# A decoder block on one core: operand start addresses, one-product sums, the start, and two groups of TensorE work moved

## What is computed

```python
xn = rmsnorm(x, norm1_g)
h  = x + mix(sig(g_conv) * conv(xn) + sig(g_attn) * attention(xn))   # conv ends in a layernorm
hn = rmsnorm(h, norm2_g)
q  = hn @ w_q                       # queries: 8 heads, 2 halves of 128
s  = einsum(q, sub_keys); top 16 of each half -> 16 of 128 x 128 experts, gate = softmax
act = gelu(u_tab[e] . hn) * gate    # 16384 experts in u_tab and v_tab
y  = h + sum(act * v_tab[e])
```

## Time and profile before

| | |
|---|---|
| median of 3 runs | 995.61 us (995.38 to 995.79) |
| the profiled execution | 996.06 us, of which the span of the trace is 994.3 us |
| TensorE busy | 989.9 us (100% of the span), 7822 records |
| VectorE, ScalarE, GpSimd busy | 773.4, 507.4, 464.6 us |
| bytes moved | 181.95 MB, mean 183 GB/s |

### The profile page before, as it was taken

One profiled execution on the slowest core, in us unless ns is written; L12 is line 12 of the kernel. 1 busy time (PEld: TensorE's weight loads), 2 busy tenths in 40 slices (PEclk: granted clock), 3 DMA queues, 4 the chain that ended last, 5 costly groups with the idle time before them and its releaser, 6 DMA issues.

```text
span 994.3 us, 21854 instructions
## 1 busy us (share of the span) xinstructions
PE 989.9 (100%) x7822; PEld 917.3 (92%) x7822; DVE 773.4 (78%) x1304; ACT 507.4 (51%) x789; POOL 464.6 (47%) x198
## 2 busy tenths in 40 slices
PE   9999999999999999999999999999999999999998
PEld 9998999999999999999999999888888888888887
DVE  6899784868899995097777777988888877676764
ACT  6654877644554444644444444444444445544443
POOL 4554466656689999874444444000000004344442
PEclk9999999999999999999999999999999999999999
DMA  7684445554455455555555545545545545555552
GB/s 263 226 272 153 147 148 183 201 191 149 161 200 190 169 211 190 190 186 177 182 176 178 177 170 170 191 169 174 180 174 174 183 171 191 191 189 199 183 206 87
DMA packets 52619, 181.95 MB, mean 183 GB/s; under 512 B 5943, under 2 KB 9155, under 8 KB 52452
## 3 DMA queue, kind: packets, MB, share of 16 engines
q1 hardware_dynamic: 52292, 181.16, 53.0%
q10 hardware_dynamic: 288, 0.27, 0.1%
HBM read 180.33 MB, written 3.43 MB: 185 GB/s over the span
## 4 chain that ended last, share of the span: by engine, by line
PE 98%; ACT 1%; DVE 0%; issue 0%; POOL 0%; ACTq 0%; POOLq 0%
PE bank L1218 53%; PE bank L1528 35%; PE bank L1477 3%; PE bank L1320 2%; PE bank L1233 1%; PE bank L1452 1%; PE bank L1242 1%; PE bank L1554 1%; PE bank L1336 1%; PE bank L1359 0%; PE bank L1347 0%; ACT hi L335 0%; DVE lo L354 0%; PE bank L1249 0%; PE bank L1297 0%; PE bank L1287 0%
## 5 line engine op out<-in xcount | busy, mean ns | idle before, releaser
L354 POOL TENSOR_TENSOR lo<-raw,hi 128x1024 fp32r<-128x1024 f32 x184 | 461.7, 2523 | 515.6 <-ACT hi L335 515.0
L335 ACT CAST hi<-raw 128x1024 fp32r<-128x1024 f32 x332 | 348.2, 1050 | 214.4 <-PE bank L1528 186.2
L1218 PE MATMUL bank<-norm_space,hi 128*128 128x256 f32 x2624 | 452.3, 278 | 0.0
L1218 PEld LDWEIGHTS bank<-norm_space,hi 128*128 128x128 f32 x2624 | 395.6, 188 | 1.5 <-issue 0.8
L1218 PE MATMUL bank<-norm_space,lo 128*128 128x256 f32 x1312 | 362.8, 277 | 0.0
L1528 PE MATMUL bank<-hi,norm_space 128*128 128x512 f32 x1008 | 273.8, 391 | 0.0
L1218 PEld LDWEIGHTS bank<-norm_space,lo 128*128 128x128 f32 x1312 | 246.4, 188 | 0.0
L1528 PEld LDWEIGHTS bank<-hi,norm_space 128*128 128x128 f32 x1008 | 187.9, 188 | 38.6
L354 DVE TENSOR_TENSOR lo<-raw,hi 128x1024 fp32r<-128x1024 f32 x148 | 187.3, 1266 | 27.2 <-ACT hi L335 27.2
L1528 PE MATMUL bank<-lo,norm_space 128*128 128x512 f32 x504 | 155.5, 390 | 0.0
L1145 DVE TENSOR_TENSOR norm_space<-act,norm_space 128x256 fp32r<-128x256 f32 x128 | 111.6, 875 | 48.8 <-ACT norm_space L665 48.8
(11 more groups left out here) (183 smaller groups left out, 653.6 us busy)
## 6 DMA issues: line engine op xcount, KB each, us to landing
raw<-u_tiles SPq DMA_DIRECT2D x128, 512.0 KB, 3.3
raw<-v_tiles SPq DMA_DIRECT2D x128, 512.0 KB, 3.3
raw<-front SPq DMA_DIRECT2D x76, 512.0 KB, 3.8
toeplitz<-bias_row SPq DMA_DIRECT2D x6, 384.0 KB, 7.4
bias<-toeplitz SPq DMA_DIRECT2D x12, 128.0 KB, 3.7
resid<-x_t SPq DMA_DIRECT2D x2, 512.0 KB, 4.8
qk<-sub_keys SPq DMA_DIRECT2D x1, 1024.0 KB, 7.5
y<-act SPq DMA_DIRECT2D x3, 256.0 KB, 2.0
```

The lines of the kernel that those rows point to most:

```text
L335: act_e.copy(hi[:, s, :], raw[:, s, :]).then_inc(hi_ready, 1)
L354: eng.tensor_tensor(lo[:, s, :], raw[:, s, :], hi[:, s, :].bitcast(F32), ALU.subtract)\
L1218: ins = pe.matmul(dst, w_[:, s, u * P:(u + 1) * P], x_[:, k, :], start=first and i == 0 and p_ == 0, stop=last and i == n - 1 and p_ == 2)
```

## The change

- **Starts.** `norm_space` loses its 8 spare floats, so that all behind it moves down by 32 bytes; `ACT_SHIFT` goes from 24 to 16 floats, and the 32 floats ahead of `rounded` are renamed. `nrm`, `act_hi`, `act_lo`, `rounded`, `hi` and `lo` now start at multiples of 64 bytes; `ksel`, `rk_parts` and `sq` start 32 bytes past one.
- **Start of the program.** The gains of the first norm are stored in front of x in `x_space` and come with its first half; ACT's transfer goes. ACT makes all eight `xg_hi`, DVE only remainders. The first tile is rounded in two halves with a counter of their own (`hi_first`), and TensorE's first products wait for the half that they read. `WARM_UP` goes from 27 to 21.
- **One product a sum.** `lnsum`, `lnvar` and `ssq2`: DVE adds the two parts first, and TensorE does one product in place of two.
- **Moves.** Both halves of the query sums now stand behind tile 16. The residual transposes stand behind the last query tile.

```diff
-SHIFT = 8
-ACT_SHIFT = 24
+ACT_SHIFT = 16
+TOKEN_SHIFT = 32
-WARM_UP = 27
+WARM_UP = 21
+X_CHUNKS = ((0, 4), (4, 8))
...
-        norm_space = sb("norm_space", [P, KB * 2 * T + SHIFT], F32R)
-        nrm = norm_space[:, SHIFT:].rearrange("p (k a t) -> p k a t", a=2, t=T)
+        norm_space = sb("norm_space", [P, KB * 2 * T], F32R)
+        nrm = norm_space[:, :].rearrange("p (k a t) -> p k a t", a=2, t=T)
...
-            a.dma_start(prm[:, C_N1:C_N1 + KB], cols[:, C_N1:C_N1 + KB]).then_inc(gain_in, 16)
             a.preload_act_table(ACT.Sqrt)
...
+            for r, (first, end) in enumerate(X_CHUNKS):
+                a.wait_ge(x_in[r], 16)
+                for k in range(first, end):
+                    a.activation(xg_hi[:, k, :], resid[:, k, :], ACT.Copy, scale=norm1_g[:, k:k + 1]).then_inc(xhi, 1)
+            wait_raw(a, 0, 0, 0)
+            a.copy(hi[:, 0, 0:D // 2], raw[:, 0, 0:D // 2]).then_inc(hi_first, 1)
+            a.copy(hi[:, 0, D // 2:D], raw[:, 0, D // 2:D]).then_inc(hi_ready, 1)
...
                     dve.tensor_tensor(sq[:, CB:CB + 2, :], acc[:, 0:2, :], acc[:, 2:4, :], ALU.add).then_inc(acc_pairs, 1)
+                    dve.wait_ge(acc_pairs, 1)
+                    dve.tensor_tensor(sq[:, CB, :], sq[:, CB, :], sq[:, CB + 1, :], ALU.add).then_inc(acc_pairs, 1)
...
+            dve.wait_ge(squared, 3 + KB)
+            dve.wait_ge(square_run, KB - 2)
+            dve.tensor_tensor(sq[:, 0, :], sq[:, 0, :], sq[:, KB - 1, :], ALU.add).then_inc(square_run, 1)
...
-                if n in (QSS_AT - 1, QSS_AT):
-                    q_sums(n - QSS_AT + 1)
+                if n == QSS_AT:
+                    for c in range(TC):
+                        q_sums(c)
...
-                    pe.wait_ge(acc_pairs, 1)
-                    for k in range(2):
-                        ins = pe.matmul(b[:, 0:T], ones[:, :], sq[:, CB + k, :], start=k == 0, stop=k == 1)
-                    step(ins)
+                    pe.wait_ge(acc_pairs, 2)
+                    step(pe.matmul(b[:, 0:T], ones[:, :], sq[:, CB, :], start=True, stop=True))
```

More of the change, by code:

```diff
@@ L380, in _ @@
         def _(sp):
-            for r in range(2):
-                sp.dma_start(resid[:, 4 * r:4 * r + 4, :], x_t[:, 4 * r:4 * r + 4, :]).then_inc(x_in[r], 16)
+            for r, (first, end) in enumerate(X_CHUNKS):
+                columns = slice(KB + first * T if r else 0, KB + end * T)
+                sp.dma_start(x_space[:, columns], x_t[:, columns]).then_inc(x_in[r], 16)
             def load(src, base, it, j):
@@ L736, in x_lo @@
                 dve.wait_ge(xhi, k + 1)
-                i, gain = k % KB, (C_N1, C_N2)[k // KB] + k % KB
-                dve.scalar_tensor_tensor(out=xg_lo[:, i, :], in0=resid[:, i, :], scalar=prm[:, gain:gain + 1],
+                i = k % KB
+                gain = prm[:, C_N2 + i:C_N2 + i + 1] if k >= KB else norm1_g[:, i:i + 1]
+                dve.scalar_tensor_tensor(out=xg_lo[:, i, :], in0=resid[:, i, :], scalar=gain,
                                          in1=xg_hi[:, i, :].bitcast(F32), op0=ALU.mult, op1=ALU.subtract)\
                    .then_inc(xlo, 1)
[L742 to L750, removed]
+            for r, (first, end) in enumerate(X_CHUNKS):
+                dve.wait_ge(x_in[r], 16)
+                for k in range(first, end):
+                    x_lo(k)
             lo_of(0)
@@ L875, in _ @@
                 if n in NORM_AT:
[L876 removed]
+                    normalise(norm1_g, 0, NORM_AT[n])
                 if n < T_QK:
@@ L1391, in _ @@
                     b = start(("lnsum",))
[L1392 to L1395 removed]
+                    pe.wait_ge(acc_pairs, 2)
+                    step(pe.matmul(b[:, 0:T], ones[:, :], sq[:, CB, :], start=True, stop=True))
                 if n == LNVAR_AT:
                     b = start(("lnvar",))
[L1398 to L1401, removed]
+                    pe.wait_ge(acc_pairs, 4)
+                    step(pe.matmul(b[:, 0:T], ones[:, :], sq[:, CB, :], start=True, stop=True))
                 if n == min(TURN_AT):
@@ L1429, in _ @@
             b = start(("ssq2",))
[L1430 to L1433, removed]
+            pe.wait_ge(square_run, KB - 1)
+            step(pe.matmul(b[:, 0:T], ones[:, :], sq[:, 0, :], start=True, stop=True))
             for u in range(2, HALVES):
                 step(full(T_WQ + u, ("wq", u), xg_hi, xg_lo))
[L1436 to L1443, removed]
-                    ins.then_inc(y_began, 1)
-            assert done[0] == FRONT_STEPS
+            assert done[0] == FRONT_STEPS
+            freed(pe, ("mix", KB - 1))
+            for c in range(TC):
+                for k in range(KB):
+                    ins = pe.matmul(bank[2 * c + k // 4][:, (k % 4) * P:(k % 4 + 1) * P],
+                                    resid[:, k, c * P:(c + 1) * P], ident[:, :], is_transpose=True,
+                                    start=k % 4 == 0, stop=False, skip_group_check=True)
+            ins.then_inc(y_began, 1)
             pe.wait_ge(sk_in, 16)
```

25 lines of the change are left out of this document (15 added, 10 removed).

## The result

The changed kernel takes 997.91 us (median of 11 runs, 996.42 to 999.80), the kernel before 995.57 us in the same comparison (995.37 to 997.28). The ratio is 1.0022 with a 95% interval of 1.0014 to 1.0029: 0.2% slower, 2.3 us, where 3.6 us less were forecast. The profiled execution took 998.22 us, its span is 996.4 us.

A forecast was written before the change was run, and what follows sets the result against it. TensorE was taken as the bound, busy 989.9 of 994.3 us. From 996.06, -0.8 - 1.3 - 1.5 - 0.1 = -3.7 gave 992.4 for an execution like the profiled one, 992.0 for the median; 8-in-10 range 962 to 999.

The forecast's parts named there:

- the cover of the add ahead of `lnvar`: DVE's added add, 0.41 us, would end near 131.4, before TensorE comes after 133, so it costs nothing.
- Start: Program start: six fewer warm-up products, TensorE begins near 9.1, short wait at first sum of squares; -0.8 us, bounds 0.3 to 1.1.
- One product a sum: `lnsum`, `lnvar` and `ssq2` lose one product of 0.43 us each, DVE's adds covered: -1.3 us.
- Residual transposes: Moved, they no longer cut the query tiles, so 312 products can keep the fast pace: -1.5 us.
- The faster stretch: Query tiles behind `ssq2`: 312 products gain 4.4 ns each, 1.4 us; nothing if the stretch restarts slow.
- Query sums: Both halves in one place save one restart: -0.1 us.
- The starts: Operands beginning at multiples of 64 bytes change nothing: 0 us, by the rule of 16-byte lines and a short row.
- the starts quicken the stream: Rival: the new starts speed TensorE's U and V products, 8 to 19 us and 18 us; chance 0.20.
- The long U stretch falls to the slow pace: Rival: 1440 U products behind the scores restart slow, 6.3 us more, 998.3; chance of slow stretches 0.22.
- The change doesn't give what it says: Rival: query stretch restarts slow (+1.4), first sum-of-squares wait takes most of the start's gain (+0.5): 994 us; chance 0.18.
- What would show it: Signs in the chain, such as starts near 9.1 and 15.1; TensorE waits among the three sums would prove the forecast wrong.

The follow-up runs named there:

- starts_only: The kernel before with only the starts moved to multiples of 64 bytes (norm_space without its spare floats): 995.65 us.
- qsums_only: The kernel before with only the query sums changed, both halves behind tile 16: 996.39 us.
- before_apart: The kernel before with only `lo` begun 128 bytes later for front and U tiles: 994.06 us.
- after_apart: The changed kernel with only `lo` begun 128 bytes later for front and U tiles: 996.10 us.

## Why the prediction was wrong

It forecast 992.0 us, faster by over 0.2%; measured were 997.91 and 0.2% slower. The range, 962 to 999, held the time by luck: its upper end was set for the long U stretch at the slow pace, and that stretch stayed fast. Two steps failed: the cover of the add ahead of `lnvar`, and the cover that the residual transposes gave. A third cost, the clock behind the query sums, was not in the sum. Step by step:

- **Start, -0.8 forecast**: right. The products began at 8.72 (9.1 forecast), `ssq1` at 14.58 after a short wait (15.1). The 1.2 us between the two profiles lie above the upper bound of 1.1, but the kernel before is not fixed there: in four traces with the old start (before, starts_only, qsums_only, before_apart) the first product begins at 9.23 to 10.17, right behind the last warm-up product, and those products go from 0.21 us apart to 0.11 at 5.4 to 7.5 us, in each execution at another time. The forecast read the latest of the four. In ten traces with the new start the warm-up ends earlier than the operands come, and the first product begins at 8.61 to 8.85. At the fourth tile the means are 19.0 and 18.3, 0.7 us apart.
- **One product a sum, -1.3 forecast**: 0.43 each came at `lnsum` and `ssq2`. At `lnvar` it cost 1.2 net. The step that failed is the cover: the add was priced at 0.41 us from L972, which reads one operand from a bank, while the added one reads both from SBUF beside GpSimd, and took 2.52. And the `lo` half "that starts 0.1 later" is a whole remainder that itself had to get in between GpSimd's subtractions; its row in the trace of before has 2.97 us, where the same instruction takes 1.22 in the earlier trace rows. It ended 2.8 us later than before. The text followed it to its own reader, 10 us on, and not to what VectorE has queued behind it: the probabilities and `pT`, for which TensorE waited 1.3 us.
- **Residual transposes, -1.5 forecast**: +1.5 came, by the wait. The step that failed is the question of who is late next: the transposes were taken for work that cuts the stream, and the chain over ScalarE and VectorE that they covered, from `ssq2` to the first freed bank, was not followed. It is 4.4 us long (210.44, where `ssq2` begins, to 214.88, where the first scaling ends); the third query tile covers 2.8 of them, and the 1.75 of the transposes covered the rest. The faster stretch did not come either.
- **Query sums, -0.1 forecast**: 1.1 to 1.5 lost in most executions. The clock was not weighed at all for a change that looked like one restart less. In the changed kernel it fell in 9 of 11 executions.
- **The starts, 0 forecast**: right by the time, and right to doubt; the reason was another. The text compared the starts with 64 bytes. What counts is the distance of weights and activations, and that did not change. By the rule of the Trainium skill weighed there (page "SBUF — State Buffer", section "Specifications (TRN2)": lines of 16 bytes) the shift changes nothing, and starts_only agrees. But the rule doesn't give the three paces: every distance that was tried begins such a line.
- **The rivals**: "the starts quicken the stream" is dead. "The long U stretch falls to the slow pace" was the right mechanism and price (6.3; 6.38 measured in two other kernels), but not what made this one slow: its U stretch was fast in the trace, and by the times in every execution. "The change doesn't give what it says" was nearest, with one of its two mechanisms: the query stretch stayed slow.
- **What would show it**: the text said that waits among the sums would prove it wrong. They did, one for `pT` behind `lnvar` and one behind `ssq2`.

What stays open: why one cut at 64 bytes leads to 113.3 and another to 117.8, when both are kept for 1440 products; and why the clock falls behind a row of 24 records in some executions and not in others.

## What to carry to other kernels

Before you move work out of a place, follow from there the chain that other engines run meanwhile, to the next thing that TensorE needs: work that looks like an interruption may be the cover. Price an added VectorE instruction from a row with the same kind of operands and the same neighbour on GpSimd, and add what it pushes behind the next GpSimd instruction. And when small undoings change a time by several us, read the long stretches by length over count first: a stretch with two paces must be made one-paced before anything of an us can be measured.

## What the runs showed that was not expected

- TensorE's rounded products of 256 columns have a pace that depends on where the weights begin against the activations, modulo 256 bytes: 113.3 to about 121 ns with nothing else running on the core. At 64 bytes there are two paces, 4% apart, and the first few products behind a cut choose for the rest of the stretch.
- A VectorE add of two SBUF operands took 2.52 us in place of 0.43 beside a GpSimd subtraction of 2.58.
- A row of 12 two-column products (24 records), 2.8 us of TensorE that the profile counts as busy, was followed by a granted clock of 0.51 for 3 us in the profiled execution of the changed kernel, and by 1.00 in that of after_apart; two rows of half the length, a tile apart, were followed by 1.00.
